# Forty of a layer's sixty-two convolution taps as TensorE products with diagonal matrices instead of VectorE multiply-adds

## Chip, cores and metric

The kernel runs on one core of one Trainium2 chip. The metric is device time in microseconds (us) of one execution, the median of several runs. "Page" below is the profile page of one profiled execution; times in a trace are counted from the start of its span.

## What is computed

A decoder trunk of two layers over 256 tokens of width 1024, all float32. Each layer has a mixer with three head groups, then a feed-forward part (dense in the first layer, top-2 of 8 experts in the second). Of the mixer this matters:

```python
proj = h @ w_in          # conv_in | c_q | c_kv | k_r | d_q | d_k | d_v
def conv_module(a, ...):
    a = a + b_glu
    u = a[..., :256] * sigmoid(a[..., 256:])
    c = depthwise causal convolution of u, width 31, one filter per channel, + b_dw
    c = silu(layer_norm(c, ln_g, ln_b))
    return c @ w_pw + b_pw
y = concatenate([conv, mla_attention (6 heads), diff_attention (6 heads)]) @ w_out
x = x + y
```

A depthwise tap is u, shifted by w tokens, times one number per channel. Channels lie on partitions, so 256 channels are two chunks c = 0, 1 of 128 x 256 elements, and a layer has 2 x 31 = 62 taps.

## The kernel before, in words

Every engine runs a program written out by hand, in order, and all waiting is by semaphores. Large weights stream from HBM in pieces of 128 x 2048 float32. ScalarE rounds each piece to fp32r (`split` in its program, L690), VectorE subtracts to get the rest (L1005), and TensorE multiplies high and low parts in three products (`mm3`, L1478 to L1480). Both rings of split pieces hold three.

A layer's mixer has two stretches. In the **projection loop** (`for p in range(NIN)`, nine pieces) TensorE runs `project(p)` and, after some pieces, small float32 products of the latent path: after p = 4 the sums of squares, after p = 5 the query products with `w_uq` (L1575), which wait for the three VectorE instructions of `latents` (L1147, L1150), after p = 6 to 8 values, rotations, keys and the first attention scores. ScalarE copies each result out of its bank (`proj_evac`). The gated input `u_pad` of the convolution is ready after p = 1 (`glu`, L1140). From then on VectorE adds taps in every p, as many as `TAPS_AT` says: 31 of chunk 0 into `cv` and 9 of chunk 1 into `tap1`, one instruction each (L1120, L1122, L1126). GpSimd does the other 22 of chunk 1 (L629, L631). `join_taps` (L1133) adds the two parts of chunk 1.

In the **slot loop** (`for k in range(SLOTS + 3)`, L1184 and others) twelve heads go through: slots 0 to 5 are the six differential heads with two score units each, slots 6 to 11 the six latent heads with one. The steps of slot k lie on all three engines:

- TensorE, iteration k: `scores(k + 2)` (L1556, L1557), `values(k - 1)` (L1633 to L1637), `transposes(k)` (L1615).
- VectorE, iteration k: `maxima(k)` (L1184), a copy of the transposed tile of slot k - 2 (L1245), `combine(k - 1)` (L1201 to L1209).
- ScalarE, iteration k: `exponentials(k)` (L756, L758), for slots 6 and up `copy_transposed(k - 2)` (L765), and `scale(k - 1)` (L770, L771), for which `transposes(k - 1)` on TensorE waits.

The layer norm and the silu of the convolution are placed in single iterations of the slot loop (`if k == 4`, `if k == 5`, ...), and `w_pw` (L1672) follows on TensorE in iteration 12. The output projection starts in iteration 11; from there to the end of the layer TensorE has work all the time.

Of the kernel before, what the change touches and what calls it, by code (L numbers as in the profile page):

```python
# [22 lines left out]
ALU = mybir.AluOpType  # L23
# [7 lines left out]
P = 128  # L31
# [69 lines left out]
CA = 5  # L101
CS_U = 3
POOL_TAPS = 22
CS_TAPS = CS_U - 1 + TAPS + (TAPS - POOL_TAPS) + 1
# [97 lines left out]
def build(nc, a, out):  # L202
    with ExitStack() as ctx:
# [137 lines left out]
        tap1 = spare[:, 6 * P:6 * P + 2 * T].rearrange("p (s t) -> p s t", s=2)  # L341
# [10 lines left out]
        dist = tabs[:, K_DIST:K_DIST + 3 * P]  # L352
        cos = tabs[0:QD, K_COS:K_COS + T]
# [49 lines left out]
        pool_taps = sem("pool_taps")  # L403
        GROUPS = ("conv", "diff", "mla")
# [276 lines left out]
        def _(act):  # L681
# [40 lines left out]
            for l in range(LAYERS):  # L722
# [49 lines left out]

                for p in range(NIN):
                    act.wait_ge(piece_used, in_done(l, p))
                    b = bank[4 + p % 4]
# [72 lines left out]
                    if p == 7:  # L848
                        exponentials(0)
                scale(0)  # L850
                for k in range(SLOTS + 3):
# [36 lines left out]
                    if k == 5:  # L888
                        act.wait_ge(conv_step, CS * l + CS_CENTRED)
                        A(glu_e[:], cv[:, 1], ACT.Square).then_inc(conv_act, 1)  # L890
                    if k == 7:
                        mid(14)
                        A(ln_rs[:], bank[7][:, 0:T], ACT.Ln, scale=1.0 / CONV, bias=eps_ln[:]).then_inc(conv_act, 1)
                        act.wait_ge(conv_act, CA * l + 3)
                        A(ln_rs[:], ln_rs[:], ACT.Exp, scale=-0.5).then_inc(conv_act, 1)
                    if k == 9:
# [102 lines left out]
        def _(dve):  # L999
# [61 lines left out]
            for l in range(LAYERS):  # L1061
# [43 lines left out]
                tap_list = []  # L1105
                for w in range(TAPS):
                    tap_list.append((0, w))
                    if w < TAPS - POOL_TAPS:
                        tap_list.append((1, POOL_TAPS + w))
                last_tap = {}  # L1110

                def taps(count):
                    for c, w in tap_list[:count]:
                        win = u_pad[:, c, w:w + T]
                        wc = dw[:, c, TAPS * l + w:TAPS * l + w + 1]
                        b = V_BDW + 2 * l + c
                        if c in last_tap:
                            dve.wait_ge(conv_step, last_tap[c])
                        if w == 0:
                            conv(V.tensor_scalar(cv[:, 0, c, :], win, wc, vecs[:, b:b + 1], ALU.mult, ALU.add))  # L1120
                        elif c not in last_tap:
                            conv(V.tensor_scalar(tap1[:, w % 2, :], win, wc, None, ALU.mult))  # L1122
                        else:
                            out, old = (tap1[:, w % 2, :], tap1[:, (w + 1) % 2, :]) if c else \
                                       (cv[:, w % 2, 0, :], cv[:, (w + 1) % 2, 0, :])
# [86 lines left out]
                for p in range(NIN):  # L1212
# [23 lines left out]
                    taps(TAPS_AT[p])  # L1236

                for k in range(SLOTS + 3):
# [28 lines left out]
                    if k == 1:  # L1267
                        join_taps()
# [9 lines left out]
                    if k == 4:  # L1278
# [3 lines left out]
                    if k == 8:  # L1282
# [589 lines left out]
```

## Time and profile before

| | us |
|---|---|
| median of 3 runs | 1316.73 (1315.9 to 1316.75) |
| the profiled execution, its own time | 1313.38 |
| span in that profile | 1311.6 |
| mean granted TensorE clock | 0.976 of full speed |
| busy in the span: TensorE, VectorE, ScalarE, GpSimd | 1243.0, 1021.0, 822.2, 144.9 |

The last instruction ends 1311.6 us after the first; the launch adds 1.8 us in this execution. The mixers of the two layers take from about 15 to 149 us and from 350 to 489 us of the span; the dense feed-forward part lies between them, and the experts fill the rest. A TensorE record's duration is that of one pass through the pipeline; products follow each other faster than that, so the price of a product is read from the starts.

### The profile page before, as it was taken

How to read it: one execution, taken by the hardware profiler on the slowest of the kernel's cores; microseconds unless marked ns; L12 is line 12 of the kernel's file. 1: busy time of each engine (PE TensorE's matmuls, PEld its weight loads, DVE VectorE, ACT ScalarE, POOL GpSimd, SP SyncE). 2: the span in 40 equal slices, each digit the busy share in tenths (PEclk: the TensorE clock that was granted, in tenths of full speed). 3: DMA queues.
4: the chain of work that ended last, by engine and by line, in shares of the span. 5: the costliest groups of instructions: out<-in, count | busy, mean ns of one | idle time of the engine just before them, and what ended most of it. 6: DMA issues, size and time to landing. Idle time of an engine off the chain costs nothing.

```text
span 1311.6 us, 18352 instructions
## 1 busy us (share of the span) xinstructions
PE 1243.0 (95%) x6658; PEld 1051.2 (80%) x6658; DVE 1021.0 (78%) x1107; ACT 822.2 (63%) x862; POOL 144.9 (11%) x139
## 2 busy tenths in 40 slices
PE   6897999999899888999999999999999999999997
PEld 6866799999787676888888888888888888888885
DVE  5985655445678747888888888988988988988986
ACT  5366544443544745777777777777777776777774
POOL 2860000000068001000000000000000000000000
PEclk9989899999999797999999999999999999999998
DMA  9400665655452039999999999999999999999961
GB/s 332 156 10 1 226 198 192 191 179 181 125 165 76 6 105 393 379 361 354 351 363 355 350 362 355 350 361 355 349 363 356 350 359 361 347 360 362 342 236 48
DMA packets 176165, 349.64 MB, mean 267 GB/s; under 512 B 5719, under 2 KB 63637, under 8 KB 176116
## 3 DMA queue, kind: packets, MB, share of 16 engines
q1 hardware_dynamic: 173852, 341.27, 73.3%
q0 software_dynamic: 2064, 7.17, 1.5%
q8 instruction: 31, 0.51, 0.2%
q10 hardware_dynamic: 200, 0.54, 0.1%
q14 instruction: 18, 0.15, 0.0%
HBM read 346.87 MB, written 2.10 MB: 266 GB/s over the span
## 4 chain that ended last, share of the span: by engine, by line
PE 84%; DVE 8%; ACT 4%; issue 3%; DMA 0%; SPq 0%; POOL 0%; DVEq 0%; ACTq 0%; POOLq 0%
PE bank L1478 26%; PE bank L1480 25%; PE bank L1479 25%; PE bank L1793 1%; DVE cv L1126 1%; ACT hi_ring L696 1%; DVE lo_ring L1005 1%; PE bank L1575 1%; DVE xn L1126 1%; PE bank L1785 1%; ACT hi_ring L690 1%; PE bank L1786 1%; PE bank L1759 1%; PE bank L1615 1%; ACT e_sb L758 1%
## 5 line engine op out<-in xcount | busy, mean ns | idle before, releaser
L1010 DVE TENSOR_TENSOR lo_ring<-raw_m,hi_ring 128x2048 fp32r<-128x2048 f32 x168 | 383.0, 2288 | 54.9 <-ACT hi_ring L696 54.8
L696 ACT ACTIVATE hi_ring<-raw_m 128x2048 fp32r<-128x2048 f32 x168 | 323.0, 1923 | 83.0 <-PE bank L1480 83.0
L1478 PE MATMUL bank<-hi_ring,hT_hi 128*128 128x512 f32 (+2 forms) x896 | 337.7, 377 | 3.4 <-DVE hT_lo L1457 3.4
L1480 PE MATMUL bank<-hi_ring,hT_lo 128*128 128x512 f32 (+2 forms) x896 | 329.7, 368 | 0.0
L1479 PE MATMUL bank<-lo_ring,hT_hi 128*128 128x512 f32 (+2 forms) x896 | 329.4, 368 | 0.0
L1010 DVE TENSOR_TENSOR lo_ring<-raw_a,hi_ring 128x2048 fp32r<-128x2048 f32 x96 | 219.9, 2291 | 41.5 <-ACT hi_ring L696 41.4
L696 ACT ACTIVATE hi_ring<-raw_a 128x2048 fp32r<-128x2048 f32 x96 | 184.2, 1919 | 62.3 <-PE bank L1480 62.3
L1005 DVE TENSOR_TENSOR lo_ring<-raw_a,hi_ring 128x2048 fp32r<-128x2048 f32 (+2 forms) x59 | 132.2, 2246 | 93.9 <-ACT hi_ring L690 93.9
L1478 PEld LDWEIGHTS bank<-hi_ring,hT_hi 128*128 128x128 f32 x896 | 169.9, 190 | 34.8 <-DVE hT_lo L1457 6.4
L1480 PEld LDWEIGHTS bank<-hi_ring,hT_lo 128*128 128x128 f32 x896 | 169.7, 189 | 29.1
L1479 PEld LDWEIGHTS bank<-lo_ring,hT_hi 128*128 128x128 f32 x896 | 170.0, 190 | 27.1 <-issue 0.5
L1478 PE MATMUL bank<-hT_hi,hi_ring 128*128 128x256 f32 (+1 forms) x576 | 165.6, 288 | 1.5 <-DVE hT_lo L1040 1.5
L1479 PE MATMUL bank<-hT_lo,hi_ring 128*128 128x256 f32 (+1 forms) x576 | 164.3, 285 | 0.0
L1480 PE MATMUL bank<-hT_hi,lo_ring 128*128 128x256 f32 (+1 forms) x576 | 164.2, 285 | 0.0
L690 ACT ACTIVATE hi_ring<-raw_a 128x2048 fp32r<-128x2048 f32 (+2 forms) x59 | 109.9, 1862 | 69.1 <-PE bank L1480 62.6
L1478 PE MATMUL bank<-hi_ring,m_hi 128*128 128x512 f32 x352 | 140.2, 398 | 5.5 <-DVE m_lo L1436 5.5
L1479 PE MATMUL bank<-lo_ring,m_hi 128*128 128x512 f32 x352 | 139.4, 396 | 0.0
L1480 PE MATMUL bank<-hi_ring,m_lo 128*128 128x512 f32 x352 | 139.4, 396 | 0.0
L1478 PEld LDWEIGHTS bank<-hT_hi,hi_ring 128*128 128x128 f32 (+1 forms) x576 | 111.5, 194 | 2.7 <-issue 2.1
L1479 PEld LDWEIGHTS bank<-hT_lo,hi_ring 128*128 128x128 f32 (+1 forms) x576 | 111.6, 194 | 0.5
L1480 PEld LDWEIGHTS bank<-hT_hi,lo_ring 128*128 128x128 f32 (+1 forms) x576 | 111.4, 193 | 0.0
L652 POOL TENSOR_TENSOR pool_pad<-half_neg 128x1 f32<-128x1 f32 x8 | 17.3, 2157 | 753.7 <-DVE slot_i L1454 753.7
(277 smaller groups left out, 1399.4 us busy)
## 6 DMA issues: line engine op xcount, KB each, us to landing
raw_m<-in_w_down_exp SPq DMA_DIRECT2D x80, 1024.0 KB, 5.2
raw_a<-in_w_up_exp SPq DMA_DIRECT2D x48, 1024.0 KB, 5.3
raw_m<-in_w_gate_exp SPq DMA_DIRECT2D x48, 1024.0 KB, 5.5
raw_a<-in_w_gate_exp SPq DMA_DIRECT2D x40, 1024.0 KB, 5.5
raw_m<-in_w_up_exp SPq DMA_DIRECT2D x40, 1024.0 KB, 5.9
raw_a<-in_w_in SPq DMA_DIRECT2D x12, 1024.0 KB, 6.6
raw_a<-in_w_gate_dense SPq DMA_DIRECT2D x11, 1024.0 KB, 5.3
raw_a<-in_w_up_dense SPq DMA_DIRECT2D x11, 1024.0 KB, 5.5
```

Source lines behind the costliest of these rows:

```text
L652: nc.gpsimd.tensor_tensor(pool_pad[:], half_neg[:], half_neg[:], ALU.mult).then_inc(pad_done, 1)
L690: A(hi_of(n)[:, 0:w], t[:, 0:w], ACT.Copy).then_inc(hi_ready, 1)
L696: A(hi_of(NA + j), t, ACT.Copy).then_inc(hi_ready, 1)
L758: A(e[:, P:3 * P], s_sb[:, u % 3, P:3 * P], ACT.Exp, scale=-1.0, bias=neg_max[:, u, 1:2], accum_out=row_sum[:, u, 1:2]).then_inc(exp_done, 1)
L1005: V.tensor_tensor(lo_of(n)[:, 0:w], raw_slot(n)[0][:, 0:w], hi_of(n)[:, 0:w].bitcast(F32), ALU.subtract).then_inc(lo_ready, 1)
L1010: V.tensor_tensor(lo_of(NA + j), expert_slot(i, j)[0], hi_of(NA + j).bitcast(F32), ALU.subtract).then_inc(lo_ready, 1)
L1126: conv(V.scalar_tensor_tensor(out, win, wc, old, ALU.mult, ALU.add))
L1478: M(o, lh, rh, start=start, stop=False)
L1479: M(o, lh, rl, start=False, stop=False)
L1480: return M(o, ll, rh, start=False, stop=stop)
L1575: r = M(bank[1 + r3][0:QD, hh * T:(hh + 1) * T], w_uq[:, c, h * QD:(h + 1) * QD], cq[:, c, :], start=c == 0, stop=c == 1)
L1615: r = nc.tensor.transpose(bank[T_BANK[k % 2]][:, b * P:(b + 1) * P], e_sb[:, k % 3, 0, b * P:(b + 1) * P], ident)
```

## The change

VectorE's 40 taps of each layer go. For tap m of 40, ScalarE writes the diagonal matrix ident x (the tap's column of weights), 128 x 128, into one of five tiles `diag[m % 5]`, and TensorE multiplies it with the shifted window of `u_pad` and accumulates in bank 7: chunk 0 in its first half, the 9 taps of chunk 1 in the second. The taps go in eight groups of five. TensorE runs group g after `project(5 + g)` for g = 0 to 3, and in slot iterations 0 to 3 for g = 4 to 7. ScalarE builds group g at the end of its iterations p = 4 + g, and groups 5, 6, 7 at the end of slot iterations 0, 1, 2; from the sixth matrix on it waits until the product of five taps earlier has read the tile. Bank 7 is taken for this from p = 5 on, so that the pieces and the scores use other banks (`IN_BANK`, `S_BANK`). ScalarE copies chunk 0 out with the bias, `join_taps` moves from slot iteration 1 to 5, and the layer norm steps move later. GpSimd's 22 taps stay.

```diff
-S_BANK, T_BANK, O_BANK = (5, 6, 4), (3, 0), (1, 2)
-OUT_BANK = (5, 6, 4, 3)
-TAPS_AT = [0, 0, 8, 9, 8, 7, 5, 2, 1]
+IN_BANK = (4, 5, 6, 7, 4, 5, 6, 4, 5)
+S_BANK, T_BANK, O_BANK = (6, 4, 5), (3, 0), (1, 2)
+OUT_BANK = (6, 4, 5, 3)
+PE_TAPS = [(0, w) for w in range(TAPS)] + [(1, w) for w in range(POOL_TAPS, TAPS)]
+TAP_GROUP = 5
+DIAGS = 5
...
+        diag = [dist[:, m * P:(m + 1) * P] for m in range(3)] + \
+               [spare[:, 6 * P + 4 * T + m * P:6 * P + 4 * T + (m + 1) * P] for m in range(2)]
...
@@ ScalarE
+                def diagonals(g):
+                    for m in range(TAP_GROUP * g, TAP_GROUP * (g + 1)):
+                        c, w = PE_TAPS[m]
+                        if m >= DIAGS:
+                            act.wait_ge(tap_mm, len(PE_TAPS) * l + m - DIAGS + 1)
+                        A(diag[m % DIAGS], ident, ACT.Copy, scale=dw[:, c, TAPS * l + w:TAPS * l + w + 1]
+                          ).then_inc(diag_set, 1)
...
+                    if p >= 4:
+                        if l == 0 and p == 4:
+                            act.wait_ge(setup_v, SETUP_V)
+                        diagonals(p - 4)
...
                     if 2 <= k <= HEADS:
                         scale(k - 1)
+                    if k < 3:
+                        diagonals(5 + k)
...
                     if k == 5:
+                        act.wait_ge(tap_mm, len(PE_TAPS) * (l + 1))
+                        A(cv[:, 0, 0, :], bank[7][:, 0:T], ACT.Identity,
+                          bias=vecs[:, V_BDW + 2 * l:V_BDW + 2 * l + 1]).then_inc(conv_act, 1)
+                    if k == 8:
                         act.wait_ge(conv_step, CS * l + CS_CENTRED)
                         A(glu_e[:], cv[:, 1], ACT.Square).then_inc(conv_act, 1)
-                    if k == 7:
+                    if k == 9:
...
-                    if k == 9:
+                    if k == 10:
                         act.wait_ge(conv_step, CS * l + CS_NORMED)
...
-                    if k == 10:
+                    if k == 11:
...
@@ VectorE
-                            conv(V.scalar_tensor_tensor(out, win, wc, old, ALU.mult, ALU.add))
...
-                    taps(TAPS_AT[p])
...
-                    if k == 1:
+                    if k == 5:
                         join_taps()
-                    if k == 4:
+                    if k == 7:
...
-                    if k == 8:
-                        dve.wait_ge(conv_act, CA * l + 4)
+                    if k == 10:
+                        dve.wait_ge(conv_act, CA * l + 5)
...
-                    if k == 11:
+                    if k == 12:
...
@@ TensorE
+                def taps(g):
+                    for m in range(TAP_GROUP * g, TAP_GROUP * (g + 1)):
+                        c, w = PE_TAPS[m]
+                        if m == 0:
+                            pe.wait_ge(conv_step, CS * l + CS_U - 1)
+                        pe.wait_ge(diag_set, len(PE_TAPS) * l + m + 1)
+                        M(bank[7][:, c * T:(c + 1) * T], diag[m % DIAGS], u_pad[:, c, w:w + T],
+                          start=m in (0, TAPS), stop=m in (TAPS - 1, len(PE_TAPS) - 1)).then_inc(tap_mm, 1)
+
                 for p in range(NIN):
                     project(p)
+                    if p >= 5:
+                        taps(p - 5)
...
                     if k >= 1:
                         values(k - 1)
+                    if k < 4:
+                        taps(4 + k)
                     if k < SLOTS:
                         transposes(k)
-                    if k == 2:
+                    if k == 6:
                         pe.wait_ge(conv_step, CS * l + CS_TAPS)
+                        pe.wait_ge(conv_act, CA * l + 2)
...
-                    if k == 5:
-                        pe.wait_ge(conv_act, CA * l + 2)
+                    if k == 8:
+                        pe.wait_ge(conv_act, CA * l + 3)
```

The order of the instructions shows two places. The first is TensorE at slot iterations 1 and 2 of the first layer, before the change (L1556 and L1557 are scores, L1633 to L1637 values, L1615 transposes):

```order
L1556 MATMUL bank<-dqk 128x128 [waits s_max]
L1557 MATMUL bank<-dqk 128x256
L1556 MATMUL bank<-dqk 128x128 [waits s_max]
L1557 MATMUL bank<-dqk 128x256
L1633 MATMUL bank<-xn,dv 128x256 [waits const_set,pt_diff]
L1634 MATMUL bank<-xn,dv 128x128
L1615 MATMUL bank<-consts,e_sb 128x128 [waits scaled_diff]
L1615 MATMUL bank<-consts,e_sb 128x128 x2
```

and the same place after it (scores are L1554 and L1555 there, values L1642 and L1643, transposes L1624, taps L1563):

```order
L1554 MATMUL bank<-dqk 128x128 [waits s_max]
L1555 MATMUL bank<-dqk 128x256
L1554 MATMUL bank<-dqk 128x128 [waits s_max]
L1555 MATMUL bank<-dqk 128x256
L1642 MATMUL bank<-xn,dv 128x256 [waits const_set,pt_diff]
L1643 MATMUL bank<-xn,dv 128x128
L1563 MATMUL bank<-u_pad,tabs 128x256 [waits diag_set] x3
L1563 MATMUL bank<-u_pad,xn 128x256 [waits diag_set] x2
L1624 MATMUL bank<-consts,e_sb 128x128 [waits scaled_diff]
L1624 MATMUL bank<-consts,e_sb 128x128 x2
```

Five products stand between the values and the transposes of the same iteration. The second place is ScalarE over slot iterations 1 and 2, before:

```order
L756 ACTIVATE e_sb,row_sum<-s_sb,neg_max 128x128 [waits s_max]
L758 ACTIVATE e_sb,row_sum<-s_sb,neg_max 128x256
L756 ACTIVATE e_sb,row_sum<-s_sb,neg_max 128x128 [waits s_max]
L758 ACTIVATE e_sb,row_sum<-s_sb,neg_max 128x256
L770 ACTIVATE e_sb<-e_sb,coef 128x128 [waits comb_done]
L771 ACTIVATE e_sb<-e_sb,coef 128x256
```

and after, from the end of iteration 1 to the end of iteration 2 (L784 builds the diagonals in `tabs` and `xn`, L762 and L764 are the exponentials, L776 and L777 the scaling):

```order
L784 ACTIVATE tabs<-consts,dw 128x128 [waits tap_mm] x3
L784 ACTIVATE xn<-consts,dw 128x128 [waits tap_mm] x2
L762 ACTIVATE e_sb,row_sum<-s_sb,neg_max 128x128 [waits s_max]
L764 ACTIVATE e_sb,row_sum<-s_sb,neg_max 128x256
L762 ACTIVATE e_sb,row_sum<-s_sb,neg_max 128x128 [waits s_max]
L764 ACTIVATE e_sb,row_sum<-s_sb,neg_max 128x256
L776 ACTIVATE e_sb<-e_sb,coef 128x128 [waits comb_done]
L777 ACTIVATE e_sb<-e_sb,coef 128x256
L784 ACTIVATE tabs<-consts,dw 128x128 [waits tap_mm] x3
L784 ACTIVATE xn<-consts,dw 128x128 [waits tap_mm] x2
```

Ahead of the exponentials of an iteration now stand five builds that wait for TensorE's products.

## Rows read from the trace of the kernel before

**Rows 1.** The page: busy time by engine, and the chain that ended last.
```profile
PE 1243.0 (95%) x6658; PEld 1051.2 (80%) x6658; DVE 1021.0 (78%) x1107; ACT 822.2 (63%) x862; POOL 144.9 (11%) x139
PE 84%; DVE 8%; ACT 4%; issue 3%; DMA 0%; SPq 0%; POOL 0%; DVEq 0%; ACTq 0%; POOLq 0%
```

**Rows 2.** Windows, columns: length; busy PE, PEld, DVE, ACT, POOL; PEclk, DMA, GB/s.
```profile
15.30:85.30 70.00, 66.26 (x495) 60.39 (x494) 62.61 (x94) 35.70 (x57) 47.19 (x40) 1.00 0.51 165
85.30:122.60 37.30, 28.00 (x151) 20.20 (x152) 29.25 (x128) 29.36 (x103) 2.79 (x4) 0.89 0.00 1
...
350.00:422.30 72.30, 69.22 (x494) 62.71 (x494) 58.32 (x80) 32.82 (x50) 48.05 (x42) 0.95 0.37 116
422.30:463.10 40.80, 31.83 (x153) 22.87 (x152) 29.75 (x128) 29.36 (x103) 2.16 (x3) 0.79 0.08 28
```

**Rows 3.** Waits of PE, 15 to 123 us, then 350 to 463 us.
```profile
PE bank L1575 <- DVE ckv L1150: 3.7, 1, 3.7
...
PE bank L1575 <- DVE ckv L1150: 3.0, 1, 3.0
```

**Rows 4.** Windows with L1575 alone: PE, PEld busy, PEclk, in either layer.
```profile
51.50:61.00 9.50, 5.39 (x24) 3.83 (x24) 1.00 0.34 113
387.50:398.00 10.50, 7.08 (x24) 4.79 (x24) 0.84 0.30 101
```

**Rows 5.** Timeline of PE, start and duration, first layer, slot iterations 0 and 3.
```profile
85.02 0.27 PE L1480 MATMUL bank<-hi_ring,hT_lo 128*128 128x192 f32 x1
85.93 0.52 PE L1556 MATMUL bank<-dqk 32*128 32x128 f32 x6 [0.64 <-ACT dv L805]
...
88.38 0.48 PE L1556 MATMUL bank<-dqk 32*128 32x128 f32 x2 [1.50 <-DVE neg_max L1184]
...
89.23 0.55 PE L1615 MATMUL bank<-consts,e_sb 128*128 128x128 f32 x3
...
98.42 0.50 PE L1556 MATMUL bank<-dqk 32*128 32x128 f32 x4
...
99.28 0.70 PE L1681 MATMUL bank<-xn,consts 128*128 128x256 f32 x2
99.82 0.59 PE L1633 MATMUL bank<-xn,dv 128*128 128x256 f32 x2
...
100.47 0.49 PE L1615 MATMUL bank<-consts,e_sb 128*128 128x128 f32 x3
```

**Rows 6.** The same, second layer: end of piece 8, transposes of slots 0 and 3.
```profile
422.05 0.28 PE L1480 MATMUL bank<-hi_ring,hT_lo 128*128 128x192 f32 x1
...
427.33 0.90 PE L1615 MATMUL bank<-consts,e_sb 128*128 128x128 f32 x3
...
441.36 0.85 PE L1615 MATMUL bank<-consts,e_sb 128*128 128x128 f32 x3
```

**Rows 7.** Timeline of ACT, first layer: one slot's exponentials, then scaling.
```profile
90.13 0.39 ACT L756 ACTIVATE e_sb<-s_sb,neg_max 128x128 f32<-128x128 f32 x1
...
91.95 0.40 ACT L770 ACTIVATE e_sb<-e_sb,coef 128x128 f32<-128x128 f32 x1
...
92.66 0.39 ACT L756 ACTIVATE e_sb<-s_sb,neg_max 128x128 f32<-128x128 f32 x1
```

**Rows 8.** Transposes at full clock, and VectorE's copy of their result.
```profile
103.83 0.55 PE L1615 MATMUL bank<-consts,e_sb 128*128 128x128 f32 x3 [1.30 <-ACT e_sb L771]
...
104.42 0.56 DVE L1245 COPY xn<-bank 128x384 f32<-128x384 f32 x1 [1.18 <-PE bank L1615]
```

**Rows 9.** L1126 by source: count, then shortest, median, longest ns.
```profile
L1126 DVE SCALAR_TENSOR_TENSOR cv<-u_pad,dw,cv x60: 472/583/966, 39.3 to 424.7; 128x256 f32<-128x256 f32 x60
```

**Rows 10.** Windows of 5 us, columns as in rows 2, each soon after a wait of TensorE.
```profile
55.00:60.00 5.00, 4.79 (x22) 3.67 (x23) 4.79 (x9) 1.19 (x2) 4.55 (x6) 1.00 0.37 148
...
430.00:435.00 5.00, 5.00 (x20) 3.50 (x21) 3.78 (x21) 3.75 (x15) 0.00 (x0) 0.50 0.00 0
```

**Rows 11.** Timeline of ACT, first layer: the second sigmoid of the convolution.
```profile
118.08 0.72 ACT L740 ACTIVATE glu_e<-glu_e,ones 128x512 f32<-128x512 f32 x1
...
119.36 0.39 ACT L756 ACTIVATE e_sb<-s_sb,neg_max 128x128 f32<-128x128 f32 x1
```

More of the change, by code:

```diff
@@ L97 @@
 SLOTS = 2 * HEADS
-S_BANK, T_BANK, O_BANK = (5, 6, 4), (3, 0), (1, 2)
-OUT_BANK = (5, 6, 4, 3)
-TAPS_AT = [0, 0, 8, 9, 8, 7, 5, 2, 1]
-CA = 5
+IN_BANK = (4, 5, 6, 7, 4, 5, 6, 4, 5)
+S_BANK, T_BANK, O_BANK = (6, 4, 5), (3, 0), (1, 2)
+OUT_BANK = (6, 4, 5, 3)
+CA = 6
 CS_U = 3
 POOL_TAPS = 22
-CS_TAPS = CS_U - 1 + TAPS + (TAPS - POOL_TAPS) + 1
+PE_TAPS = [(0, w) for w in range(TAPS)] + [(1, w) for w in range(POOL_TAPS, TAPS)]
+TAP_GROUP = 5
+DIAGS = 5
+CS_TAPS = CS_U
 CS_CENTRED = CS_TAPS + 1
@@ L403, in build @@
         pool_taps = sem("pool_taps")
+        diag_set = sem("diag_set")
+        tap_mm = sem("tap_mm")
         GROUPS = ("conv", "diff", "mla")
@@ L771, in scale @@
                     A(e[:, P:3 * P], e[:, P:3 * P], ACT.Copy, scale=coef[:, u, 1:2]).then_inc(scaled_diff, 1)
+                def diagonals(g):
[5 more added lines that the diff above has]
+                          ).then_inc(diag_set, 1)
                 for p in range(NIN):
                     act.wait_ge(piece_used, in_done(l, p))
-                    b = bank[4 + p % 4]
+                    b = bank[IN_BANK[p]]
                     if p == 0:
@@ L1101, in mids @@
                     ins.then_inc(mid_dve, 1)
[L1105 to L1125, printed above, removed]
-                            conv(V.scalar_tensor_tensor(out, win, wc, old, ALU.mult, ALU.add))
-                        last_tap[c] = cs[0]
-                    del tap_list[:count]
                 def join_taps():
                     dve.wait_ge(pool_taps, POOL_TAPS * (l + 1))
-                    dve.wait_ge(conv_step, cs[0])
-                    conv(V.tensor_tensor(cv[:, 0, 1, :], cv[:, (POOL_TAPS - 1) % 2, 1, :], tap1[:, (TAPS - 1) % 2, :],
-                                         ALU.add))
+                    dve.wait_ge(tap_mm, len(PE_TAPS) * (l + 1))
+                    dve.wait_ge(conv_act, CA * l + 2)
+                    conv(V.tensor_tensor(cv[:, 0, 1, :], bank[7][:, T:2 * T], cv[:, (POOL_TAPS - 1) % 2, 1, :], ALU.add))
                 def glu():
@@ L1519, in project @@
                     if p >= 4:
-                        pe.wait_ge(proj_evac, NIN * l + p - 3)
+                        pe.wait_ge(proj_evac, NIN * l + (p - 2 if p >= 7 else p - 3))
                     elif l == 0 and p in (0, 3):
                         pe.wait_ge(setup_a, 1 if p == 0 else 2)
-                    b = bank[4 + p % 4]
+                    b = bank[IN_BANK[p]]
                     wh, wl = in_piece_view(hi_of(n), p), in_piece_view(lo_of(n), p)
@@ L1542, in scores @@
                     for u in units_of(k):
-                        if u == 0:
-                            pe.wait_ge(proj_evac, NIN * l + 7)
+                        if u <= 1:
+                            pe.wait_ge(proj_evac, NIN * l + 7 + u)
                         if u == 2:
```

3 lines of the change are left out of this document (1 added, 2 removed).

## The prediction

> **What bounds the kernel now.** I read the page first: TensorE is busy 95% of the span and is 84% of the chain that ended last [rows 1]. So time that is added to TensorE's program is lost, unless it falls into one of its waits; time taken from VectorE is won only where TensorE waits for VectorE. The windows by stage show where such waits are [rows 2]. In the projection loops TensorE is busy 66.3 of 70.0 us and 69.2 of 72.3 us. In the slot loops it is busy 28.0 of 37.3 us and 31.8 of 40.8 us, with VectorE and ScalarE busy 29 us each: there the three engines pass work round, and no engine alone sets the pace. The list of waits names what the VectorE taps cost in the projection loop: L1575 waits 3.7 us and 3.0 us for the latents, which stand behind a batch of taps [rows 3]. In the second layer the clock is also down after that wait: L1575 takes 7.08 us instead of 5.39 us [rows 4].
>
> **Price of a tap.** VectorE gives up 40 instructions a layer of 0.58 us in the median [rows 9], 23 us. ScalarE gets 40 diagonals: 128x128 with a scale per partition, as L770, whose successor starts 0.3 us later; 12 us a layer. TensorE gets 40 float32 products of 128x128 with 128x256. The nearest row is L1575, also float32 with 256 columns and another stationary tile each time. The program has 12 products there and the trace 24 records, two for each; they take 5.39 us, so one costs 0.45 us at full clock [rows 4], a group of five 2.25 us and a layer's 40 taps 18 us. The lower bound is one record's share, 0.22 us; the upper is L1575 at the fallen clock, 0.59 us. I take 0.45 us, since width, type and number of records are the same.
>
> **Projection loop.** Three groups stand before piece 8 ends: +6.75 us. The wait for the latents goes, since without the taps VectorE is at them before piece 5 is through: -3.7 us in the first layer, -3.0 and -1.7 us (the fallen clock) in the second. That is +3.0 and +2.05 us. ScalarE is busy 36 of 70 us here [rows 2], and each group is built a piece before it is used, so the builds are hidden; if that cover were gone they would cost 1.5 us a group. From the end of piece 8 to the transposes of slot 0 it was 3.9 us (85.3 to 89.2) and 5.0 us (422.3 to 427.3) [rows 5, 6]. Now it is group 3 (2.25), the scores (three units 0.9, about 0.5 for the maximum that the last one needs, 0.9 for the last) and group 4 (2.25), 6.8 us: +2.9 and +1.8 us. The transposes of slot 0 come 5.9 and 3.9 us later than before.
>
> **Slot loop, the step that decides.** ScalarE's program is in order. At the end of iteration 1 it builds group 6, each matrix waiting for a product of group 5; group 5 stands on TensorE behind `values(0)`, and that behind VectorE's copy. Ahead of the transposes of slot 1 ScalarE still has the exponentials of slot 2 and the scaling of slot 1 to do. So what ran side by side becomes a ring. Counted from the end of a tap group: last build 0.45 us (L770's record 0.40), exponentials 1.8 us (90.13 to 91.95), scaling 0.75 us (91.95 to 92.66) [rows 7], hand-over 0.05: transposes at 3.05 us. Then transposes 0.45 (a record 0.55, less overlap), scores 0.86 (98.42 to 99.28), values 0.65 (99.82 to 100.47) [rows 5], taps 2.25: a turn of 7.3 us. VectorE's copy starts 0.59 us after the transposes and takes 0.56 us [rows 8], within transposes and scores. The first turn, group 4 to group 5, goes otherwise: build 0.45, one pair of exponentials 0.9, maximum 0.6, copy 0.56 and hand-over 0.1, then values and taps, 5.5 us. With slot 0's transposes at 0: group 5 ends at 5.5, transposes 1 at 8.55, group 6 ends at 12.8, transposes 2 at 15.8; in iteration 3 the product L1681 (0.54) waits for a square that ScalarE does after one more set of exponentials, to 18.6; values 0.65 and group 7 bring the transposes of slot 3 to 21.5 us. Before, the same stretch took 11.2 us (89.23 to 100.47) and 14.0 us (427.33 to 441.36) [rows 5, 6]: +10.3 and +7.5 us.
>
> **The rest.** The steps of the layer norm move from iterations 1 to 11 to 5 to 12. The second sigmoid, 1.3 us between two sets of exponentials [rows 11], gets behind the start of the output projection; against that, the steps of iteration 10 now follow each other on VectorE and ScalarE within one iteration. I take 0, with -2.6 and +4 us over both layers as bounds (the sigmoid gone in each; 2 us of direct waiting in each). After the slot loop TensorE is without a long wait, and the loads of the experts are released by steps of this chain, so a delay arrives at the end in full.
>
> **The clock.** The ring gives TensorE two waits of about 3 us a layer. Of the two waits of that length in the trace one was followed by the full clock (1.00 in 55 to 60 us [rows 10]), the other cost 1.7 us [rows 4]. Four waits at half of 1.7 us: +3.4 us.
>
> **Sum.** 5.9 + 10.3 + 3.9 + 7.5 + 3.4 = +31 us. The profiled execution, 1313.4 us, becomes 1344.4 us. The median of the runs is 3.35 us above it: **1347.8 us**.
>
> **Rivals.**
> *The ring does not hold ScalarE up.* Then the pace of slots 1 to 3 is the busiest engine's: TensorE 2.25 + 0.45 + 0.86 + 0.65 = 4.2 us against 1.8 + 0.7 + 1.5 = 4.0 us on ScalarE; with L1681 13 us for three slots, +1.8 and -1.0 us. With 5.9 and 3.9 us that is +10.6 us, 1327 us. For it speaks that all matrices of a group are ready before the group starts; against it the order of the two programs, which leaves the builds ahead of the exponentials.
> *The clock stays down in the ring.* The second layer shows how: at 0.50 from 430 us on, though TensorE is busy all of the window [rows 10]. Products, values, scores and transposes on the ring come to 12.3 us a layer and double: 27.6 + 24.6 = +52 us, 1369 us. Against it: most waits of the slot loops leave the clock up. The Trainium skill (TensorE: Matmul & The Clock Gate, HAM oscillation) says that waits between bursts of products let the clock fall back each time; by that this case would be the likely one, and only the second layer's 0.50 bears it out.
> *The taps are cheap and fill waits: faster.* If a product costs what one record does, 0.22 us, the 25 taps before slot 0 cost 5.6 us a layer less, and if the ring also does not hold, ScalarE sets 4.0 us a slot: +1.1 and -3.7 us, and the sigmoids off the chain -2.6 us. That is -5.2 us, 1311.5 us; with a free ring the sign turns at about 0.26 us a product. Against it stand the two records of each product in L1575.
> The Trainium skill (same page, Back-to-back issue gap) gives N/2.4 ns and some 2.5 ns, an estimate of 0.11 us for 256 columns; by it this case would give 1306 us. The rows for float32 are four times that.
>
> **Chances.** The ring as summed 0.60 (own range 1338 to 1357 us), ring free 0.22 (1321 to 1338), clock down 0.09, cheap taps 0.06, and 0.03 that gains and losses cancel to within 0.2%. 0.2% (2.6 us) is about what a measurement of this kernel can tell from no change. Faster 0.06, same 0.03, slower 0.91. The range, 1325 to 1360 us, holds the first case, most of the second and a start of the third. It takes in 0.40 to 0.50 us a tap and both bounds of the rest.
>
> **What would show it.** TensorE: 80 products of L1563 as 160 records, some 0.45 us apart; no wait before the `w_uq` products; transposes of slot 0 at about 95 us, of slot 3 at about 117 us. ScalarE: builds that wait for the taps in slot iterations 0 to 2, and exponentials right behind them. VectorE some 46 us less busy. The prediction is wrong if the transposes of slots 1 to 3 follow each other at 4 to 5 us, if a product takes under 0.3 us, or if the slot loops end less than 8 us later than before.

## The result, and the profile after

The changed kernel takes 1369.28 us (median of 4 runs, 1365.12 to 1369.92) against 1316.32 us of the kernel before beside it (4 runs, 1314.19 to 1316.75): a ratio of 1.0402, 95% interval 1.0383 to 1.0421, so 4% slower. The profiled execution took 1368.97 us with a span of 1367.2 us, 55.6 us longer than before. The direction was as predicted; the size was not, since the range ended at 1360 us.

The page of the changed kernel, busy time by engine and the chain that ended last, answers to [rows 1]:

```profile
PE 1289.9 (94%) x6818; PEld 1090.5 (80%) x6818; DVE 972.4 (71%) x1027; ACT 850.6 (62%) x944; POOL 138.4 (10%) x139
PE 90%; ACT 4%; DVE 3%; issue 2%; DMA 0%; SPq 0%; POOL 0%; ACTq 0%; DVEq 0%; POOLq 0%
```

VectorE lost 48.6 us of busy time and its share of the chain fell from 8% to 3%; TensorE gained 46.9 us and went from 84% to 90%. The tap products and their neighbours on TensorE, first layer (start, duration, as in [rows 5]):

```profile
51.76 1.46 PE L1563 MATMUL bank<-u_pad,tabs 128*128 128x256 f32 x6
53.05 1.03 PE L1563 MATMUL bank<-u_pad,xn 128*128 128x256 f32 x4
53.92 5.34 PE L1584 MATMUL bank<-cq,w_uq 128*96 128x256 f32 x24
...
95.17 0.49 PE L1624 MATMUL bank<-consts,e_sb 128*128 128x128 f32 x3
...
97.96 1.02 PE L1642 MATMUL bank<-xn,dv 128*128 128x256 f32 x2 [1.44 <-DVE xn L1243]
...
99.21 2.65 PE L1563 MATMUL bank<-u_pad,tabs 128*128 128x256 f32 x6
101.70 1.03 PE L1563 MATMUL bank<-u_pad,xn 128*128 128x256 f32 x4
105.66 0.90 PE L1624 MATMUL bank<-consts,e_sb 128*128 128x128 f32 x3 [2.94 <-ACT e_sb L777]
...
109.52 2.62 PE L1563 MATMUL bank<-u_pad,tabs 128*128 128x256 f32 x6
111.97 1.03 PE L1563 MATMUL bank<-u_pad,xn 128*128 128x256 f32 x4
115.94 0.90 PE L1624 MATMUL bank<-consts,e_sb 128*128 128x128 f32 x3 [2.94 <-ACT e_sb L777]
```

A group of five is ten records and takes 2.16 us (51.76 to 53.92), 0.43 us a product. The query products follow it with no wait; before they had one of 3.7 us [rows 3]. Slot 0's transposes stand at 95.17 us, where 95 us was foretold. Then the ring: after group 5 and after group 6 TensorE waits 2.94 us each time for ScalarE's scaling (L777). The first six records of a group take 2.65 and 2.62 us there instead of the 1.46 us at 51.76: the clock is down. At 99.21 it is down already, behind the wait of 1.44 us and ahead of the first ring wait. In the second layer the same wait left it up:

```profile
464.73 0.70 PE L1642 MATMUL bank<-xn,dv 128*128 128x256 f32 x2 [1.44 <-DVE xn L1243]
...
465.49 1.46 PE L1563 MATMUL bank<-u_pad,tabs 128*128 128x256 f32 x6
```

ScalarE in the same stretch of the first layer, where L784 builds a diagonal and L762, L764 are the exponentials:

```profile
100.31 0.40 ACT L784 ACTIVATE tabs<-consts,dw 128x128 f32<-128x128 f32 x1 [2.78 <-PE bank L1563]
101.16 0.40 ACT L784 ACTIVATE tabs<-consts,dw 128x128 f32<-128x128 f32 x1 [0.45 <-PE bank L1563]
...
102.33 0.83 ACT L784 ACTIVATE xn<-consts,dw 128x128 f32<-128x128 f32 x2
103.07 0.39 ACT L762 ACTIVATE e_sb<-s_sb,neg_max 128x128 f32<-128x128 f32 x1
...
104.82 0.39 ACT L776 ACTIVATE e_sb<-e_sb,coef 128x128 f32<-128x128 f32 x1
...
110.62 0.40 ACT L784 ACTIVATE tabs<-consts,dw 128x128 f32<-128x128 f32 x1 [5.01 <-PE bank L1563]
```

The builds follow the tap products one by one, and the exponentials of the next slot come behind the last build. ScalarE waits 2.78 and 5.01 us for taps here, and then TensorE waits 2.94 us for ScalarE. These are the two halves of the ring. Windows of the changed kernel, columns as in [rows 2], first the ring by 5 us, then slots 0 to 3 and 3 to 10 of either layer:

```profile
95.00:100.00 5.00, 3.56 (x19) 2.62 (x18) 2.72 (x13) 2.50 (x10) 0.00 (x0) 0.82 0.01 3
...
105.00:110.00 5.00, 4.34 (x17) 3.09 (x18) 2.17 (x9) 0.60 (x2) 0.00 (x0) 0.50 0.00 0
110.00:115.00 5.00, 3.00 (x10) 2.16 (x8) 0.54 (x3) 3.57 (x12) 0.00 (x0) 0.81 0.00 0
115.00:120.00 5.00, 4.06 (x15) 2.81 (x16) 2.82 (x15) 4.31 (x18) 0.00 (x0) 0.53 0.00 0
```

```profile
95.20:123.50 28.30, 20.99 (x78) 15.41 (x77) 8.89 (x43) 16.54 (x61) 0.00 (x0) 0.70 0.00 1
123.50:151.60 28.10, 19.19 (x86) 14.27 (x85) 16.05 (x65) 16.16 (x50) 0.00 (x0) 0.84 0.00 1
461.90:488.70 26.80, 19.49 (x78) 14.26 (x77) 8.89 (x43) 16.60 (x61) 0.00 (x0) 0.75 0.00 1
488.70:516.80 28.10, 19.16 (x86) 14.27 (x85) 16.02 (x65) 16.17 (x50) 0.00 (x0) 0.84 0.00 1
```

After either ring wait the granted clock is down (0.50 from 105 to 110 us, 0.53 from 115 to 120 us; 0.50 is 1.2 GHz), and it comes back before the next one (0.81 from 110 to 115 us, 1.00 from 112 to 113). In slots 3 to 10 no engine is busy more than 19.2 of 28.1 us, so none of them sets the pace alone. The kernel before, slots 0 to 3 of either layer and 3 to 10 of the first:

```profile
89.23:100.47 11.24, 10.83 (x53) 7.64 (x52) 9.29 (x45) 8.95 (x38) 0.00 (x0) 0.70 0.00 0
100.47:122.13 21.66, 14.91 (x84) 11.02 (x82) 15.91 (x68) 17.96 (x59) 0.00 (x0) 0.99 0.00 2
427.33:441.36 14.03, 14.03 (x52) 9.71 (x52) 9.59 (x44) 9.72 (x40) 0.00 (x0) 0.50 0.00 0
```

From slot 3 to 10 the clock was 0.99 before and is 0.84 now. TensorE's idle time there rose from 6.8 to 8.9 us, and its busy time from 14.9 to 19.2 us.

All kernels below are read by the same marks, the start of the transposes of slots 0, 3, 10 and 11 on TensorE in either layer (read from the timelines, in us):

| kernel | slot 0, layer 1 | 0 to 3 | 3 to 10 | 10 to 11 | slot 0, layer 2 | 0 to 3 | 3 to 10 | 10 to 11 |
|---|---|---|---|---|---|---|---|---|
| before | 89.2 | 11.2 | 21.7 | 7.8 | 427.3 | 14.0 | 21.5 | 6.5 |
| after | 95.2 | 28.4 | 28.1 | 8.6 | 461.9 | 26.8 | 28.1 | 8.7 |
| e1_ten_tiles | 95.1 | 13.0 | 27.4 | 7.5 | 443.8 | 13.0 | 28.7 | 8.2 |
| e2_fill | 95.1 | 21.5 | 27.7 | 8.0 | 453.6 | 21.5 | 27.7 | 8.0 |
| e3_late_norm | 92.1 | 12.3 | 26.4 | 8.4 | 437.3 | 12.3 | 26.4 | 8.2 |
| e4_all_in_projection | 102.1 | 12.5 | 22.4 | 6.5 | 449.1 | 11.4 | 21.2 | 6.5 |
| e5_late_with_slack | 94.0 | 12.3 | 24.0 | 7.6 | 435.2 | 12.3 | 22.5 | 8.3 |
| e6_ten_and_slack | 95.2 | 13.0 | 24.6 | 7.1 | 440.3 | 13.0 | 25.0 | 8.0 |
| v0_order | 90.0 | 12.3 | 22.2 | 6.5 | 424.8 | 12.2 | 21.7 | 6.5 |
| v1_nine_taps | 90.9 | 10.1 | 22.8 | 6.5 | 426.0 | 11.5 | 21.7 | 7.7 |
| v2_more_behind | 91.6 | 12.5 | 22.4 | 6.5 | 426.7 | 12.2 | 22.2 | 6.5 |

Layer 2 of the changed kernel starts 30.9 us later than before (its projection at 380.97 instead of 350.08), so slot 0 there stands 3.7 us later in its layer. The 55.6 us are thereby found: 5.9 + 3.7 up to slot 0, 17.1 + 12.8 in slots 0 to 3, 6.4 + 6.7 in slots 3 to 10, 0.9 + 2.2 from 10 to 11, and -0.1 elsewhere. The profiled execution of the kernel before was 3.3 us below its median, so marks compared with it show a kernel some 3 us later than the medians do. A part of that lies ahead of slot 0: e3 and e5 stand at 92.1 and 94.0 us there though no step ahead of it was moved (only `tap1` lies elsewhere). The granted clock from 50 to 60 us, behind the same 3.7 us wait for the latents, is 1.00 in the profile of before and 0.83 and 0.88 in theirs.

Two things help to read the table. From slot 10 to 11 TensorE is busy all the time in every kernel, and the length follows the clock: 6.5 us at 1.00, 7.8 us at 0.82, 8.6 us at 0.73. And the first column sums of the layer norm, two float32 products of 0.87 us together (134.23 to 135.10 us after the change), lie between slots 2 and 3 before, in e4 and in the v kernels, and between slots 3 and 10 in all the others. So 0.9 us a layer of what slots 3 to 10 gain there is this work in a new place.

### The profile page after: what moved, and what is told of

The parts are those of the page before. It is cut to its first block, busy times and chain, and to the rows that moved or that the text cites. A ratio compares the mean times of both kernels' runs of the same rounds, so it can differ in the third digit from the quotient of the medians.

```text
span 1367.2 us, 18678 instructions
## 1 busy us (share of the span) xinstructions
PE 1289.9 (94%) x6818; PEld 1090.5 (80%) x6818; DVE 972.4 (71%) x1027; ACT 850.6 (62%) x944; POOL 138.4 (10%) x139
## 4 chain that ended last, share of the span: by engine, by line
PE 90%; ACT 4%; DVE 3%; issue 2%; DMA 0%; SPq 0%; POOL 0%; ACTq 0%; DVEq 0%; POOLq 0%
PE bank L1476 26%; PE bank L1478 26%; PE bank L1477 26%; PE bank L1563 3%; PE bank L1805 1%; ACT hi_ring L702 1%; PE bank L1584 1%; PE bank L1624 1%; ACT e_sb L764 1%; PE bank L1555 1%; PE bank L1771 1%; PE bank L1797 1%; ACT e_sb L762 1%; PE bank L1646 0%; PE bank L1798 0%
## 5 line engine op out<-in xcount | busy, mean ns | idle before, releaser
L1477 PEld LDWEIGHTS bank<-lo_ring,hT_hi 128*128 128x128 f32 x896 | 170.6, 190 | 27.4 <-issue 0.5
```

The costliest lines, as they stand in the source:

```text
L1477: M(o, lh, rl, start=False, stop=False)
```

## The experiments

The theory going in was the prediction's: a ring between ScalarE's builds and TensorE's taps. The trace after added two things to be told apart: the clock, and slots 3 to 10, where nothing had been forecast.

### e1_ten_tiles: the ring opened

The five further tiles lie in storage that is idle at this point.

```diff
-DIAGS = 5
+DIAGS = 10
...
+               [sq_q[:, m // 2, (m % 2) * P:(m % 2 + 1) * P] for m in range(4)] + [sq_kv[:, 0:P]]
```

> The change with ten diagonal tiles instead of five (the five new ones lie in sq_q and sq_kv, which are free by then); nothing else. Ring theory (ScalarE's builds wait for taps that stand behind ScalarE's own earlier work): the two waits of 2.9 us before the transposes of slots 1 and 2 go, and the 28.4 and 26.8 us from the transposes of slot 0 to those of slot 3 become about 14 us each, set by ScalarE (1.8 + 0.7 + 5 x 0.43 us a slot); 1342 us. Load theory (the slots are longer because TensorE and ScalarE have more to do, whatever the ring): no change, 1369 us.

Measured: 1337.25 us, ratio 1.0157 (1.0127 to 1.0186); 32 us of the 53 us are gone. Two windows of it, slots 0 to 3 and 3 to 10 of the first layer:

```profile
95.10:108.10 13.00, 13.00 (x78) 10.35 (x77) 8.16 (x39) 11.56 (x46) 0.00 (x0) 1.00 0.00 1
108.10:135.50 27.40, 18.19 (x86) 13.75 (x85) 15.99 (x65) 17.11 (x54) 0.00 (x0) 0.85 0.00 1
```

With ten tiles ScalarE is a group ahead, TensorE is busy 13.00 of 13.00 us at full clock, and three slots take 13.0 us, in the second layer too. (The expectation had ScalarE set the pace, with a build each 0.43 us. Freed from the tap products its builds start 0.30 to 0.34 us apart, three in 0.98 us at 88.67 and four in 1.42 us at 98.03, and TensorE sets it.) The work is the same; only the wait for a free tile has changed. So the ring is shown, and it costs 15.4 and 13.8 us, its share of the clock included (28.4 and 26.8 against 13.0). The rival, that the work itself fills the time, falls. The second window shows that slots 3 to 10 keep nearly all their extra time: 27.4 us where 21.7 us stood before.

### e2_fill: the ring kept, TensorE's waits filled

Fourteen products of no use go behind the taps of slot iterations 1 and 2, into a part of a bank that nothing reads then.

```diff
                     if k < 4:
                         taps(4 + k)
+                    if k in (1, 2):
+                        for _ in range(14):
+                            M(bank[T_BANK[k % 2]][:, 3 * P:4 * P], ones[:], ident, start=True, stop=True)
```

> The change with the ring as it is, and 14 useless float32 products of 128 columns (3.1 us at full clock) in each of the two waits before the transposes of slots 1 and 2. Clock theory (the waits let TensorE's clock fall, and everything after them on the ring runs at half speed): the clock stays at 1.00 through the slots 1 to 3, these take 21.5 us instead of 28.4 and 26.8, and the kernel is 12 us faster, 1357 us, though it does more. Rival (the clock falls for another reason, or its fall costs little): 1369 us or up to 6 us more.

Measured: 1355.39 us, ratio 1.0294 (1.0262 to 1.0327). TensorE has more to do, and the kernel is 13.9 us faster than the changed one. Its timeline, with L1697 the useless products:

```profile
99.90 1.02 PE L1563 MATMUL bank<-u_pad,xn 128*128 128x256 f32 x4
100.77 3.29 PE L1697 MATMUL bank<-consts,ones 128*128 128x128 f32 x28
103.89 0.52 PE L1624 MATMUL bank<-consts,e_sb 128*128 128x128 f32 x3
```

and its window, in the place of the 0.50 above:

```profile
105.00:110.00 5.00, 5.00 (x35) 4.47 (x32) 1.87 (x12) 3.28 (x12) 0.00 (x0) 1.00 0.00 0
```

The clock is 1.00, and slots 0 to 3 take 21.5 us in both layers: the ring without the clock's share. With the clock's share it took 28.4 and 26.8 us, so the clock cost 6.8 + 5.3 = 12.1 us there. Turn by turn (the starts of the transposes of both kernels), the two turns behind the ring waits are 2.9 + 2.3 us longer in the first layer and 3.0 + 2.3 us in the second, 10.4 us in all. The other 1.7 us lie in the first turn of the first layer (95.17 to 105.66 us, against 95.06 to 103.89), behind the wait of 1.44 us. The Trainium skill (TensorE: Matmul & The Clock Gate, HAM oscillation) says that waits between bursts of products let the clock fall each time; this case agrees: behind all four waits of 2.94 us the clock was near 0.50, and it was 1.00 where they are filled.

### e3_late_norm: only the moved steps

The kernel before, with all its taps on VectorE, and the layer norm steps in the iterations of the changed kernel: on ScalarE the square 8 instead of 5, Ln and Exp 9 instead of 7, the exponentials 10 instead of 9, the sigmoid 11 instead of 10; on VectorE `join_taps` 5 instead of 1, the centring 7 instead of 4, the normalizing 10 instead of 8, the last product 12 instead of 11; on TensorE the first sums 6 instead of 2, the second 8 instead of 5. The two tiles of `tap1` also move to storage in which they last until iteration 5. Three of these edits:

```diff
-                    if k == 1:
+                    if k == 5:
                         join_taps()
...
-                    if k == 4:
+                    if k == 7:
                         dve.wait_ge(mid_mm, MID * l + 14)
...
-                    if k == 2:
+                    if k == 6:
                         pe.wait_ge(conv_step, CS * l + CS_TAPS)
```

> The kernel before (VectorE does its 40 taps), with the join, the two column sums and the layer norm steps in the iterations in which the change has them (5, 6, 7, 8, 8, 9, 10, 10, 11, 12). Placement theory (each of these steps now waits directly for the one before it on another engine, and holds its engine's queue meanwhile): slots 3 to 10 take 21.7 + 5 to 6.5 us, the kernel 1327 to 1329 us. Rival (slots 3 to 10 are longer in the change only because the clock is down after the ring): 1316 to 1319 us.

Measured: 1327.33 us, ratio 1.0081 (1.0052 to 1.011). Slots 3 to 10 take 26.4 us in both layers instead of 21.7 and 21.5. So 4.7 + 4.9 us there, and 0.6 + 1.7 us from slot 10 to 11, come with the places of these steps alone, with no tap on TensorE and no ring; 0.9 us of it a layer is the product named above. The window of slots 3 to 10 in the first layer:

```profile
104.45:130.84 26.39, 19.05 (x87) 14.77 (x87) 16.16 (x65) 17.14 (x53) 0.00 (x0) 0.82 0.00 1
```

The clock is 0.82, where before it was 0.99 and TensorE was busy 14.91 us. It is also lower in the others with late steps (e5 0.86 and 0.88, e6 0.89 and 0.86, e1 0.85 and 0.83), and in e4 0.92 and 1.00. On TensorE the 4.7 us are 0.6 us more idle time and 4.1 us more busy time. So the late steps cost time in waits and in slower products together, and no run here tells the two apart.

### e4_all_in_projection: all taps early, the steps where they were

Ten tiles, two groups behind each of the pieces 5 to 8, and the layer norm steps in the iterations of the kernel before.

```diff
                     if p >= 5:
-                        taps(p - 5)
+                        taps(2 * (p - 5))
+                        taps(2 * (p - 5) + 1)
...
-                    if k < 4:
-                        taps(4 + k)
```

> The change with ten tiles, all eight groups in the projection loop (two after each of the pieces 5 to 8), and the join and norm steps in the iterations of the kernel before. If the ring and the placement are all that is wrong besides TensorE's load, what is left is that load: 18 us a layer, less the wait for the latents (3.7; 3.0 and 1.7 of fallen clock) and less the wait at the start of the slots (1.5, 1.8) and the fallen clock of the second layer's slots (2.8): +12.8 and +8.7 us, 1338 us. If a tap costs more than 0.45 us or the load is not what counts, it is off by over 5 us to one side.

Measured: 1331.94 us, ratio 1.0116 (1.0087 to 1.0146), 6 us better than expected. Slot 0 comes 12.8 us later in the first layer, and slots 3 to 10 are back at 22.4 and 21.2 us though all 40 taps are still TensorE's. That agrees with e3 on the steps' places; against e1 it moved the taps, too, but in neither kernel does a tap lie between slots 3 and 10. In the second layer slot 0 comes 10.0 us later, and slots 0 to 3 give 2.7 us back against before (11.4 instead of 14.0). Its profile ends 19.0 us later than that of before, its median 15.2 us later; most of the difference is the 3.3 us by which the profiled execution of before lay below its median. Against the 21.5 us expected the profile's 19.0 us are 2.5 us less; nearly all the rest of the 6 us is that 3.3, which the 1338 us had added.

### e5_late_with_slack and e6_ten_and_slack: late, or without slack

Why do the places cost time? The rows of the changed kernel in iterations 5 to 9, all engines, waits in brackets:

```profile
127.06 0.42 DVE L1133 TENSOR_TENSOR cv<-bank,cv 128x256 f32<-128x256 f32 x1 [1.32 <-ACT cv L910]
...
135.30 0.69 DVE L1279 SCALAR_TENSOR_TENSOR cv<-bank,cv 128x512 f32<-128x512 f32 x1 [1.22 <-PE bank L1701]
136.58 0.40 ACT L762 ACTIVATE e_sb<-s_sb,neg_max 128x128 f32<-128x128 f32 x1 [3.86 <-DVE neg_max L1183]
137.88 0.70 PE L1690 MATMUL bank<-xn,consts 128*128 128x256 f32 x2 [1.97 <-ACT xn L876]
...
143.98 0.47 ACT L917 ACTIVATE ln_rs<-bank,eps_ln 128x256 f32<-128x256 f32 x1 [2.89 <-PE bank L1706]
```

VectorE's iteration 7 waits 1.22 us for the sums of TensorE's iteration 6 (L1701), and its maxima for the next slot stand behind that. ScalarE is idle for 3.86 us until they come, and TensorE then 1.97 us for ScalarE. The 3.86 us hold more than VectorE's wait: from 132.5 us on VectorE is copying the transposed tile and dividing by the sums of its slot. VectorE and ScalarE run an iteration ahead of TensorE, so a step of theirs in iteration k + 1 that needs TensorE's k has no slack. Before, the sums stood in 2 and the centring in 4, the second sums in 5 and Ln in 7: two apart. After, 6 and 7, 8 and 9: one apart. e5 keeps the last steps as late as in e3 and puts the distance back by having the first ones earlier: `join_taps` in 3, the first sums in 4, the centring in 6, the square and the second sums in 7, Ln still in 9. Against e3_late_norm:

```diff
-                    if k == 5:
+                    if k == 3:
                         join_taps()
...
-                    if k == 7:
+                    if k == 6:
                         dve.wait_ge(mid_mm, MID * l + 14)
...
-                    if k == 6:
+                    if k == 4:
                         pe.wait_ge(conv_step, CS * l + CS_TAPS)
```

> The kernel before with the norm steps late, as in e3_late_norm (1327.3 us), but with an iteration of slack put back where the page of the changed kernel shows the waits: the join and the first pair of sums are two iterations earlier than in e3_late_norm (3 and 4), and VectorE's centring (6) and ScalarE's Ln (9) each stand two iterations behind TensorE's sums instead of one. The square, the normalizing, the exponentials, the sigmoid and the last product stay in iterations 7 to 12. If the slots lose time because the steps follow each other without slack, slots 3 to 10 take about 22.5 us again instead of 26.4 and the kernel about 1318 us. The rival is that lateness itself costs (the sigmoid and the last steps beside the start of the output projection): then slots 3 to 10 come back by under 1 us and it is 1326 us.

Measured: 1319.97 us over 10 runs, ratio 1.003 (1.002 to 1.0041), against 1.0081 for e3. Over the kernel before beside each it is 4.0 us instead of 10.6 us, and slots 3 to 10 take 24.0 and 22.5 us. The wait for the first sums (1.0 us in either layer of e3) is gone; one for the second is left in the first layer, 1.2 instead of 2.6 us:

```profile
ACT ln_rs L893 <- PE bank L1694: 1.2, 1, 1.2
```

where e3 had

```profile
ACT ln_rs L893 <- PE bank L1694: 2.6, 1, 2.6
```

e6 does it on the changed kernel, with the ten tiles of e1: ScalarE's copy of chunk 0 and `join_taps` in 4, the first sums in 5, the square and the second sums in 7. Against e1_ten_tiles:

```diff
-                    if k == 5:
+                    if k == 4:
                         join_taps()
...
-                    if k == 6:
+                    if k == 5:
                         pe.wait_ge(conv_step, CS * l + CS_TAPS)
```

> The changed kernel with ten tiles (e1_ten_tiles, 1337.3 us) and the join one iteration earlier (4), the first sums in iteration 5, the square and the second sums in iteration 7, with VectorE's centring still in 7 and Ln in 9: one iteration of slack ahead of both. Slack theory: slots 3 to 10 take some 23 us instead of 27.4 and 28.7, 1328 us; if the wait of VectorE for ScalarE's copy of chunk 0 in the join's iteration is the larger part, it stays above 26 us and 1335.

Measured: 1330.33 us, ratio 1.0111 (1.0088 to 1.0134), between the two figures of the expectation and 6.9 us below e1. Slots 3 to 10 take 24.6 and 25.0 us instead of 27.4 and 28.7. What is left is in part the join, which now waits longer for ScalarE's copy of the products of chunk 0:

```profile
DVE cv L1134 <- ACT cv L911: 3.2, 1, 3.2
```

So half or more of the loss in slots 3 to 10 goes when the distance is back (6.3 of e3's 9.6 us, 6.6 of the 13.0 us of e1), on both kernels. Of e3's share 2.4 + 1.0 us stay in e5, and 0.9 us of each is the product in its new place; of e1's 2.9 + 3.5 us stay in e6. How that is made up is open. Both runs also put the first steps one or two iterations earlier, so what the lateness of these alone costs is not shown; that of the last steps, which stayed late in e5, is at most the 4.0 us that e5 takes more than before.

### v0_order, v1_nine_taps, v2_more_behind: what the kernel before really lacked

The one gain that the change had was the wait for the latents. It can be had in other ways. v0 changes one line of the kernel before:

```diff
-TAPS_AT = [0, 0, 8, 9, 8, 7, 5, 2, 1]
+TAPS_AT = [0, 0, 8, 4, 12, 8, 5, 2, 1]
```

> The kernel before with five of VectorE's taps moved from p = 3 to p = 4, behind the latents (TAPS_AT 0 0 8 4 12 8 5 2 1); nothing goes to TensorE. If the wait for the latents is a matter of order alone, it shrinks by 3 us in each layer and the kernel takes 1310 us or so. If VectorE is loaded so fully that they are missed later (the pieces or the maxima late instead), 1316 us.

The edit moves four taps to p = 4 and one to p = 5. Measured: 1309.3 us, ratio 0.9946 (0.9929 to 0.9963), faster by more than the 0.2% that can be told, and close to the 1310 us of the order theory. v1 gives TensorE only the nine taps of chunk 1, behind piece 5, with nine tiles and no ring, and leaves the layer norm steps where they were:

```diff
-TAPS_AT = [0, 0, 8, 9, 8, 7, 5, 2, 1]
+TAPS_AT = [0, 0, 8, 9, 7, 5, 2, 0, 0]
+PE_TAPS = [(1, w) for w in range(POOL_TAPS, TAPS)]
...
                 for p in range(NIN):
                     project(p)
+                    if p == 5:
+                        taps()
```

> The kernel before with only the nine taps of chunk 1 on TensorE (all after piece 5, in nine tiles built by ScalarE before), VectorE keeps the 31 of chunk 0, 31 = 8+9+7+5+2 in p = 2 to 6; norm steps as before. If TensorE's 4.05 us of products just fill its wait for the latents (3.7 and 3.0 us, and 1.7 us of clock), and VectorE, with 5.5 us less to do, is at the maxima in time (1.5 and 1.8 us of wait go, and the fall of the clock that follows in the second layer, 2.8 us): -1.2 and -5.4 us, 1310 us. Load theory (each product costs in full): +8 us, 1324 us.

Measured: 1311.25 us, ratio 0.9963 (0.9949 to 0.9977), near the 1310 us of filled waits; the load theory's 1324 us falls. v2 is v1 with fewer taps ahead of the latents:

```diff
-TAPS_AT = [0, 0, 8, 9, 7, 5, 2, 0, 0]
+TAPS_AT = [0, 0, 8, 5, 10, 6, 2, 0, 0]
```

> v1_nine_taps (1311.25 us: 9 taps of chunk 1 on TensorE, 31 of chunk 0 on VectorE, layer norm steps where they were) with VectorE's taps as 8, 5, 10, 6, 2 instead of 8, 9, 7, 5, 2 over pieces 2 to 6, so that four fewer stand ahead of the latents. TensorE still waits 1.6 and 0.9 us there in v1. If that wait goes and nothing else is late: 1308.7 us, ratio 0.994. If VectorE's later taps only move the wait to the start of the slots: 1311 us.

Measured: 1308.16 us, ratio 0.9943 (0.9929 to 0.9958). This is nearer the 1308.7 us of the first case than the 1311 us of the second, though the intervals of v1 and v2 overlap a little. TensorE's waits of v0, 385 to 430 us, and of v2, same stretch:

```profile
PE bank L1556 <- DVE neg_max L1184: 3.8, 1, 3.8
PE bank L1556 <- ACT dv L805: 1.5, 1, 1.5
```

```profile
PE bank L1565 <- DVE neg_max L1193: 0.7, 1, 0.7
PE bank L1565 <- ACT dv L818: 0.6, 1, 0.6
```

Both have lost the wait for the latents (3.0 us there before; in the first layer 0.7 us of 3.7 is left in v0). v0 has got longer waits at the start of the slots (3.8 us for the maxima instead of 1.8) and still does all 40 taps on VectorE; v2 hasn't, but pays nine products on TensorE, 4 us a layer at 0.43 us each. The two come out alike: their intervals nearly coincide. So nothing here shows that a tap on TensorE gains anything over the order of the taps on VectorE. v0 is the change worth keeping, a line of numbers for 7 us.

## Why the prediction was wrong

| step | predicted | measured |
|---|---|---|
| a tap product | 0.45 us | 0.43 us at full clock |
| up to slot 0 | +5.9, +3.9 us | +5.9, +3.7 us |
| slots 0 to 3 at full clock | 21.5 us: +10.3, +7.5 | 21.5 us in both layers (e2_fill) |
| "The clock" | +3.4 us | +6.8, +5.3 = 12.1 us in slots 0 to 3, of which 10.4 us behind the four ring waits |
| "The rest" | 0, bounds -2.6 to +4 us | 6.4 + 6.7 + 0.9 + 2.2 = 16.2 us |
| sum | +31 us | +55.6 us of span |
| median above the profiled execution | +3.35 us | +0.3 us |

**Right.** The price of a product was taken from the nearest row with its number of records, and held. So did the projection loop, where the wait for the latents vanished and three groups came in. The ring was foretold from the order of two programs, and its turn of 7.3 us is 7.36 us in e2_fill (103.89 to 111.25). The rule of the Trainium skill with which the prediction weighed the price (TensorE: Matmul & The Clock Gate, Back-to-back issue gap), 0.11 us for 256 columns, holds in this trace for the fp32r products, which follow each other at 0.12 us, and not for plain float32. The Trainium skill (FP8 and Floating Point Precision, TensorE Precision Notes) also says that true FP32 goes through the array four times; 0.43 us against 0.12 us, 3.6 times, agrees roughly.

**The clock was mis-sized.** The prediction paid half of 1.7 us for each ring wait, 0.85 us, from one wait that had cost a stretch of ordinary work 1.7 us. The clock fell behind all four and cost 10.4 us, 2.6 us each. Behind a ring wait stand only products that are on the ring, so their slower pace is paid in full there: the group of taps at 109.52 us takes 3.5 us to the end of its last record instead of 2.3 us, and scores and values are slowed too. A fall of the clock behind the wait of 1.44 us, which the sum did not have, added 1.7 us. A step that failed is "Four waits at half of 1.7 us". The prediction also said that most waits of the slot loops leave the clock up; in slots 0 to 3 of the kernel before it was 0.70 and 0.50, and in the second layer, at 0.50 throughout and with TensorE busy all of it, that stretch took 2.8 us more than in the first (14.03 against 11.24 us).

**"The rest" was the larger miss.** The other step that failed is "I take 0, with -2.6 and +4 us over both layers as bounds"; the marks show 16.2 us. I counted where the steps went (5 to 12 instead of 1 to 11) and what they met at the end, and not how far a consumer stood behind its producer. The distance in iterations between TensorE's sums and the two steps that read them fell from two to one. With VectorE and ScalarE an iteration ahead, that is from some slack to none. The order of each engine shows it ahead of any run, and the bound of "2 us of direct waiting in each" layer left out that one engine's wait delays the two others: behind VectorE's wait of 1.22 us ScalarE stood idle for 3.86 us and TensorE for 1.97 us. Three parts of the 16.2 us can be named. The 3.1 us from slot 10 to 11 are the clock alone. Another 1.7 us are the first sums: the prediction took them out of slots 0 to 3, whose 21.5 us do not hold them, and did not add them where they went. And e3, with no tap moved, shows 11.9 of the 16.2 us, in which the 1.7 us and 2.3 of the 3.1 us lie. The other 4.3 us, which come with the taps on TensorE, have no run of their own; one thing that is new there is ScalarE's copy of chunk 0, for which `join_taps` waits 1.32 us.

**The rivals.** 1369 us was the figure of the rival in which the clock stays down, and the kernel took 1369.28 us. That is in good part chance: the clock took 12.1 us in slots 0 to 3 where that rival had 24.6 us, and slots 3 to 11, which it had at 0, took 16.2 us. The rival "the ring does not hold" had 13.0 us for three slots, which is what e1_ten_tiles measured once the ring was open. What e1 has above that rival's 1327 us is again slots 3 to 11, 14.5 us by the marks, less the 3 us that the rival had added for the median. The cheap taps fell with the first rows of L1563. ScalarE's builds cost the 0.3 us put down for them where nothing holds them (three in 0.98 us at 85.05). Where the tap products of five taps earlier are still running, they follow these, 0.43 us apart (three in 1.26 us at 88.79, beside the products from 88.13 on).

## What to carry to other kernels

A buffer ring that two in-order engines share is priced by walking one turn through both programs, with everything that stands behind the waiting instruction; more buffers, not less work, took 32 us out of this one. When steps that cross engines are moved, count the iterations between producer and consumer before and after, since a distance that fell to the lead of one engine over the other turned into waits on all three here. And before work is moved off an engine to end one wait, try its order on that engine: here three numbers in one line gained 7 us with no engine's load changed.

## What the runs showed of the hardware

Plain float32 products of 128x128 with 128x256 cost 0.43 us each at full clock. The fp32r ones of the projection, also with 256 columns, follow each other at 0.12 us (TensorE, changed kernel):

```profile
50.20 0.28 PE L1478 MATMUL bank<-hT_hi,lo_ring 128*128 128x256 f32 x1
50.32 0.28 PE L1476 MATMUL bank<-hT_hi,hi_ring 128*128 128x256 f32 x1
50.44 0.28 PE L1477 MATMUL bank<-hT_lo,hi_ring 128*128 128x256 f32 x1
```

The same work isn't granted the same clock in every execution. Up to 98 us the changed kernel and e2_fill run the same instructions, with the same wait of 1.44 us at the same place; the window from 95 to 100 us is at 0.82 in the one and this in the other:

```profile
95.00:100.00 5.00, 3.56 (x24) 2.72 (x22) 2.72 (x13) 3.11 (x12) 0.00 (x0) 1.00 0.01 3
```

So a wait of 1.44 us doesn't settle what the clock does next, and neither does the wait of 3.7 us for the latents (1.00, 0.83 and 0.88 behind it in the profiles of before, e3 and e5), and one profile of each kernel doesn't show how often it falls. That filling the waits pays is shown by the medians (1355.39 against 1369.28 us), and the split into 12.1 us of clock is that of two profiled executions.
